# Squares summed ahead of the statistics matmul, the last weight tile loaded in pieces, and a reordered ending

## The reference

```python
for layer in range(2):                       # first block, 256 tokens
    mod = silu(c) @ ada_w[layer] + ada_b[layer]
    sh1, sc1, g1, sh2, sc2, g2 = split(mod, 6)
    h = modulate(rms_norm(x, mix_norm[layer]), sh1, sc1)
    y = ab_mixer(h) if layer == 0 else cd_mixer(h)     # each ends in: mix @ w_out
    x = x + g1 * y
    h = modulate(rms_norm(x, ffn_norm[layer]), sh2, sc2)
    x = x + g2 * swiglu(h, ffn_w1[layer], ffn_w2[layer])

h = concatenate([meta_tokens, x])            # second block, 16 + 256 = 272 tokens
proj = rms_norm(h, mix_norm_g) @ w_in
attn, conv = diff_attention(...), gated_conv(...)
h = h + concatenate([attn, conv]) @ w_out
h = h + expert_choice_ffn(rms_norm(h, ffn_norm_g), w_router, w_gate, w_up, w_down)
return rms_norm(h, final_norm_g)[:, 16:, :]

def rms_norm(t, w):
    return t * rsqrt(mean(t * t, axis=-1) + 1e-6) * w
```

## Time and profile before

| | |
|---|---|
| median of 3 runs | 1895.21 us (1893.5, 1895.21, 1895.69) |
| the profiled execution | 1902.33 us, with a span of 1900.9 us |
| TensorE busy | 1677.1 us, 88% of the span |
| TensorE weight load busy | 1007.9 us, 53% |
| VectorE busy | 634.5 us, 33% |
| ScalarE busy | 373.4 us, 20% |
| GpSimd busy | 32.4 us, 2% |
| moved by DMA | 577.30 MB, mean 304 GB/s |

### The profile page before, as it was taken

The page is one execution under the profiler, slowest core; times in us unless marked ns, Lnnn a source line. Parts: engine busy times, 40 slices in busy tenths (PEclk is TensorE's granted clock), DMA queues, the critical chain, the costliest instruction groups (busy, mean ns, idle before and its releaser), DMA issues.

```text
span 1900.9 us, 20565 instructions
## 1 busy us (share of the span) xinstructions
PE 1677.1 (88%) x8771; PEld 1007.9 (53%) x8771; DVE 634.5 (33%) x1227; ACT 373.4 (20%) x648; POOL 32.4 (2%) x39
## 2 busy tenths in 40 slices
PE   3998899999889999999799988898888878888877
PEld 2775699997679999657533322233222222222222
DVE  6567277755747554253300100101001010010102
ACT  2213243432433433041101000000000000000001
POOL 0101000000000000100010000000000000000000
PEclk7989889999999999999889998999889899999999
DMA  9554248745647545222569999999999999999995
GB/s 397 232 213 181 106 175 331 256 169 207 241 155 263 184 175 222 89 89 89 221 259 415 427 430 431 422 404 424 431 431 421 431 430 424 431 422 428 431 429 231
DMA packets 43739, 577.30 MB, mean 304 GB/s; under 512 B 4721, under 2 KB 6786, under 8 KB 7298
## 3 DMA queue, kind: packets, MB, share of 16 engines
q1 hardware_dynamic: 43650, 576.00, 74.0%
HBM read 574.93 MB, written 1.05 MB: 303 GB/s over the span
## 4 chain that ended last, share of the span: by engine, by line
PE 67%; DMA 22%; DVE 8%; ACT 2%; issue 1%; SPq 0%; DVEq 0%; ACTq 0%
DMA RING_T<-in_w_up 20%; PE P L989 18%; PE P L416 13%; PE P L1010 5%; PE P L697 4%; PE P L698 4%; PE P L699 4%; PE P L718 2%; PE P L717 2%; PE P L716 2%; PE P L967 2%; PE P L425 2%; DVE RING_T L1555 2%; PE P L1026 2%; DMA RING_T<-in_ada_w 1%; PE P L443 1%
## 5 line engine op out<-in xcount | busy, mean ns | idle before, releaser
L989 PE MATMUL P<-RING_T,SCR 128*34 128x512 f32 x1008 | 483.9, 637 | 118.6 <-DMA RING_T<-in_w_up 118.6
L990 PE MATMUL P<-RING_T,SCR 128*34 128x512 f32 x992 | 477.8, 639 | 0.0
L989 PEld LDWEIGHTS P<-RING_T,SCR 128*34 128x34 f32 x1008 | 114.6, 119 | 435.4 <-issue 434.8
L2097 DVE TENSOR_TENSOR SCR<-P,SCR 34x512 f32<-34x512 f32 x64 | 44.4, 693 | 772.4 <-ACT SCR L1464 772.4
L1010 PE MATMUL P<-RING_T,SCR 128*34 128x512 f32 x512 | 227.9, 594 | 10.6 <-DMA RING_T<-in_w_down 10.6
L1011 PE MATMUL P<-RING_T,SCR 128*34 128x512 f32 x512 | 227.9, 594 | 0.0
L697 PE MATMUL P<-SCF 128*128 128x256 f32 x704 | 205.1, 291 | 15.7 <-DVE SCF L1828 11.1
L416 PE MATMUL P<-HWC,RING_T 128*128 128x256 f32 (+1 forms) x832 | 196.9, 395 | 7.9 <-ACT HWC L1108 4.1
L698 PE MATMUL P<-SCF 128*128 128x256 f32 x704 | 202.8, 288 | 0.0
L699 PE MATMUL P<-SCF 128*128 128x256 f32 x704 | 202.6, 288 | 0.0
L416 PEld LDWEIGHTS P<-HWC,RING_T 128*128 128x128 f32 x832 | 161.7, 196 | 40.6 <-issue 14.1
(11 more groups left out here) (245 smaller groups left out, 1732.8 us busy)
## 6 DMA issues: line engine op xcount, KB each, us to landing
RING_T<-in_w_down SPq DMA_DIRECT2D x64, 2048.0 KB, 13.7
RING_T<-in_w_gate SPq DMA_DIRECT2D x63, 2048.0 KB, 16.7
RING_T<-in_w_up SPq DMA_DIRECT2D x62, 2048.0 KB, 12.2
RING_T<-in_ada_w SPq DMA_DIRECT2D x24, 2048.0 KB, 10.2
RING_T<-in_ffn_w SPq DMA_DIRECT2D x22, 2048.0 KB, 8.5
RING_T<-in_ffn_w SPq DMA_DIRECT2D x22, 1024.0 KB, 4.9
RING_T<-in_ab_w_in SPq DMA_DIRECT2D x7, 2048.0 KB, 18.0
RING_T<-in_w_in SPq DMA_DIRECT2D x6, 2048.0 KB, 8.4
```

Of the source, the lines that this page charges most:

```text
L989: pe.matmul(u.t[0:CAP, :], xs, wg.v(KC, 512)[:, c, :], start=c == 0, stop=c == KC - 1)
L990: ins = pe.matmul(u.t[64:64 + CAP, :], xs, wu.v(KC, 512)[:, c, :], start=c == 0, stop=c == KC - 1)
```

## The change

Six things change.

1. In the three output projections, VectorE adds up the squares of chunks 0 to 6 in `H[:, 0]`, one addition behind each residual from the third on, and TensorE multiplies ones with that sum and with the square of chunk 7 after the last chunk (`pe_out_stat`). `PeStat` is no longer used there, and no bank is held.
2. The last down tile of the last expert is loaded by four DMAs of 512 KB, each with its own semaphore, and the last four pairs of matmuls wait for one piece each.
3. For all experts, VectorE copies the right half of the result to `Y` in ScalarE's place.
4. The last combination and its residuals work on 256 columns instead of 272.
5. ScalarE's last table load is issued before its copy of the last expert's result, in place of after the last square.
6. VectorE multiplies each chunk of the final `X` with the norm's weight into a new buffer `XF` as soon as the chunk is there, and after the reciprocal root three products (four, three and one chunk) and three output transfers follow.

```diff
+FINAL = ((0, 4), (4, 7), (7, 8))
+OUT_STATS = ["ffn0", "ffn1", "ffn2"]
...
+        self.XF = s.take(KC, T, at=s.at)
...
-def pe_out_proj(nc, k, name, keys, mix, n, stat):
+def pe_out_stat(nc, k, name, c0):
+
+    u = pe_bank(nc, k, ("rms", name))
+    nc.tensor.wait_ge(k.sem["squares"], 6 * OUT_STATS.index(name) + 6)
+    nc.tensor.matmul(u.t[:, 0:L - c0], k.cc("ones"), k.H[:, 0, c0:L], start=True, stop=False)
+    nc.tensor.wait_ge(k.sem["square"], SQ[name] + KC)
+    nc.tensor.matmul(u.t[:, 0:L - c0], k.cc("ones"), k.H[:, KC - 1, c0:L], start=False, stop=True).then_inc(u.full, 1)
+
+
+def pe_out_proj(nc, k, name, keys, mix, n):
     for i in range(2):
         w = k.ring[keys[i]]
         nc.tensor.wait_ge(w.sem, w.n)
         for j in range(4):
             u = pe_chunk(nc, k, (name, "out", 4 * i + j), w.v(KC, 512), j, mix, n)
-            stat.upto(min(max(4 * i + j - stat.lag, 0), KC) if 4 * i + j < 7 else 7)
         w.left = (u.full, u.n)
-    stat.upto(KC)
...
-    stat = PeStat(nc, k, "ffn0", M)
-    stat.lag = 2
...
-    pe_out_proj(nc, k, "ab", [("abo", 0), ("abo", 1)], v.MIX, T, stat)
+    pe_out_proj(nc, k, "ab", [("abo", 0), ("abo", 1)], v.MIX, T)
+    pe_out_stat(nc, k, "ffn0", M)
...
     def down(e, i, u):
         w = ring["d", e, i]
-        pe.wait_ge(w.sem, w.n)
+        pieces = (e, i) == (E_N - 1, 3)
+        if not pieces:
+            pe.wait_ge(w.sem, w.n)
         t = P["eturn", e, i]
         pe.wait_ge(t.taken, t.done)
         for c in range(4):
+            if pieces:
+                pe.wait_ge(s[f"last{c}"], 16)
...
-            pe.matmul(u.t[:, 0:L], v.Y[0:NP, g % 2, c * 128:(c + 1) * 128], v.OGT[0:NP, g, :], start=True, stop=True).then_inc(u.full, 1)
+            c0 = M if stat else 0
+            pe.matmul(u.t[:, 0:L - c0], v.Y[0:NP, g % 2, c * 128:(c + 1) * 128], v.OGT[0:NP, g, c0:L], start=True, stop=True).then_inc(u.full, 1)
...
+        if e == E_N - 1:
+            act_table(nc, SET_EXP)
+
         u, g, r = P["eo", e], e // 2, 64 * (e % 2)
...
         act.activation(v.Y[r:r + CAP, g % 2, 0:512], u.t[0:CAP, :], ACT.Copy).then_inc(u.taken, 1)
-        act.activation(v.Y[r:r + CAP, g % 2, 512:1024], u.t[64:64 + CAP, :], ACT.Copy).then_inc(u.taken, 1)
     for c in range(KC):
         act_square(nc, k, M, c, P["comb", 7, c])
-    act_table(nc, SET_EXP)
     act_stat(nc, k, "fin", M)
...
-def dve_out_proj(nc, k, name, n, c0, gate):
+def dve_out_proj(nc, k, name, n, c0, gate, stat):
+
+    s, done = k.sem, 6 * OUT_STATS.index(stat)
     for c in range(KC):
         u = k.banks[name, "out", c]
         nc.vector.wait_ge(u.full, u.n)
         dve_residual(nc, k, u, u.t[:, 0:n], c, c0, gate)
+        if c >= 2:
+            nc.vector.wait_ge(s["square"], SQ[stat] + c)
+            if c > 2:
+                nc.vector.wait_ge(s["squares"], done + c - 2)
+            nc.vector.tensor_tensor(k.H[:, 0, c0:L], k.H[:, 0, c0:L], k.H[:, c - 1, c0:L], ALU.add).then_inc(s["squares"], 1)
...
+    def weighed(c):
+
+        u = P["comb", 7, c]
+        dve.wait_ge(u.taken, u.done)
+        dve.tensor_scalar(v.XF[:, c, :], k.X[:, c, M:L], k.vv("fin", c, c + 1), None, ALU.mult).then_inc(s["weighed"], 1)
+
...
-    combine(7)
+        u, g, r = P["eo", e], e // 2, 64 * (e % 2)
+        dve.wait_ge(u.full, u.n)
...
+        dve.tensor_copy(v.Y[r:r + CAP, g % 2, 512:1024], u.t[64:64 + CAP, :]).then_inc(u.taken, 1)
+    for c in range(KC):
+        u = P["comb", 7, c]
+        dve.wait_ge(u.full, u.n)
...
+        dve_residual(nc, k, u, u.t[:, 0:T], c, M, None)
+        if c:
+            weighed(c - 1)
+    weighed(KC - 1)
     dve_stat(nc, k, "fin", M)
-    dve_normed(nc, k, "fin", M, k.vv("fin"))
+    dve.wait_ge(s["weighed"], KC)
+    dve.wait_ge(s["rs"], rms_done("fin"))
+    for a, b in FINAL:
+        dve.tensor_tensor(v.XF[:, a:b, :], v.XF[:, a:b, :], bc(k.RS[:, 0:1, 0:T], b - a, T), ALU.mult).then_inc(s["final"], 1)
...
+    w = k.ring["d", E_N - 1, 3]
+    sp.wait_ge(*w.prev.left)
+    for c in range(4):
+        sp.dma_start(w.t[:, c * D:(c + 1) * D], A["w_down_2"][E_N - 1, 3][:, c * D:(c + 1) * D]).then_inc(s[f"last{c}"], 16)
     od = k.out.rearrange("p (k t) -> p k t", k=KC)
-    for c in range(0, KC, 4):
-        sp.wait_ge(s["hn"], HN["fin"] + c + 4)
-        sp.dma_start(od[:, c:c + 4, :], k.H[:, c:c + 4, M:L]).then_inc(s["out"], 16)
-    sp.wait_ge(s["out"], 32)
+    for n, (a, b) in enumerate(FINAL):
+        sp.wait_ge(s["final"], n + 1)
+        sp.dma_start(od[:, a:b, :], k.ex.XF[:, a:b, :]).then_inc(s["out"], 16)
+    sp.wait_ge(s["out"], 16 * len(FINAL))
```

More of the change, by code:

```diff
@@ L225 @@
 SEMS = [
-    "vecs", "cond_in", "ones_in", "consts", "x", "pos", "narrow", "small", "gup", "later", "poolw", "ex0", "ex1", "ex2", "out",
-    "cond", "ada", "mod", "xr", "xr_p", "sa", "square", "ln", "rs", "hs", "hn",
+    "vecs", "cond_in", "ones_in", "consts", "x", "pos", "narrow", "small", "gup", "later", "poolw", "ex0", "ex1", "ex2", "last0", "last1", "last2", "last3", "out",
+    "cond", "ada", "mod", "xr", "xr_p", "sa", "square", "squares", "ln", "rs", "hs", "hn",
     "angle", "trig", "g1one", "iwt", "gate_a", "gate_d", "decay_a", "decay_d", "cosm", "rope", "qeke", "kdqd", "atzero", "at", "relu", "score",
@@ L238 @@
     "lam_d", "lam_a", "dcos", "drope", "amax", "aexp", "asoft", "osq", "osub", "onorm", "czero", "conv",
-    "wkzero", "rmax", "rexp", "raff", "rtop", "rmask", "rank", "onehot", "ogzero", "og", "yzero", "esilu", "edown",
+    "wkzero", "rmax", "rexp", "raff", "rtop", "rmask", "rank", "onehot", "ogzero", "og", "yzero", "esilu", "edown", "weighed", "final",
 ]
@@ L790, in pe_cd @@
         pe.matmul(u.t[:, 0:T], v.PW[:, g, :], v.W4[g][:, g, M:L], start=True, stop=True).then_inc(u.full, 1)
-    stat = PeStat(nc, k, "ffn1", M)
-    stat.lag = 2
     for i in range(4):
@@ L796, in pe_cd @@
         pe.wait_ge(P["pooled", i].taken, P["pooled", i].done)
-    pe_out_proj(nc, k, "cd", [("cdo", 0), ("cdo", 1)], v.MIX, T, stat)
+    pe_out_proj(nc, k, "cd", [("cdo", 0), ("cdo", 1)], v.MIX, T)
+    pe_out_stat(nc, k, "ffn1", M)
 def pe_diff(nc, k):
@@ L899, in pe_diff @@
         chunk("cb", j)
-    stat = PeStat(nc, k, "ffn2", 0)
-    stat.lag = 0
     pe.wait_ge(s["onorm"], 4)
@@ L905, in pe_diff @@
         pe.wait_ge(t.taken, t.done)
-    pe_out_proj(nc, k, "diff", [("o2", 0), ("o2", 1)], v.MIX, L, stat)
+    pe_out_proj(nc, k, "diff", [("o2", 0), ("o2", 1)], v.MIX, L)
+    pe_out_stat(nc, k, "ffn2", 0)
 def pe_experts(nc, k):
@@ L1786, in dve_ab @@
     dve.wait_ge(s["mod"], ADA_AT[0, 5] + 1)
-    dve_out_proj(nc, k, "ab", T, M, k.gate(0, 0))
+    dve_out_proj(nc, k, "ab", T, M, k.gate(0, 0), "ffn0")
 class DveLow:
@@ L1919, in dve_cd @@
     dve.wait_ge(s["mod"], ADA_AT[1, 5] + 1)
-    dve_out_proj(nc, k, "cd", T, M, k.gate(1, 0))
+    dve_out_proj(nc, k, "cd", T, M, k.gate(1, 0), "ffn1")
 def dve_diff(nc, k):
@@ L2030, in dve_diff @@
         convolved(j)
-    dve_out_proj(nc, k, "diff", L, 0, None)
+    dve_out_proj(nc, k, "diff", L, 0, None, "ffn2")
 def dve_experts(nc, k):
@@ L2125, in dve_experts @@
         turned(e, 3)
-    combine(7)
+        u, g, r = P["eo", e], e // 2, 64 * (e % 2)
+        dve.wait_ge(u.full, u.n)
+        if e == 0:
+            dve.wait_ge(s["yzero"], 1)
+        if g >= 2:
+            t = P["comb", g - 2, KC - 1]
+            dve.wait_ge(t.full, t.n)
+        dve.tensor_copy(v.Y[r:r + CAP, g % 2, 512:1024], u.t[64:64 + CAP, :]).then_inc(u.taken, 1)
+    for c in range(KC):
+        u = P["comb", 7, c]
+        dve.wait_ge(u.full, u.n)
+        if c == 0:
+            t = P["comb", 6, KC - 1]
+            dve.wait_ge(t.taken, t.done)
+        dve_residual(nc, k, u, u.t[:, 0:T], c, M, None)
+        if c:
+            weighed(c - 1)
+    weighed(KC - 1)
     dve_stat(nc, k, "fin", M)
-    dve_normed(nc, k, "fin", M, k.vv("fin"))
+    dve.wait_ge(s["weighed"], KC)
+    dve.wait_ge(s["rs"], rms_done("fin"))
+    for a, b in FINAL:
+        dve.tensor_tensor(v.XF[:, a:b, :], v.XF[:, a:b, :], bc(k.RS[:, 0:1, 0:T], b - a, T), ALU.mult).then_inc(s["final"], 1)
 def vector_program(nc, k):
```

3 lines of the change are left out of this document (2 added, 1 removed).

## The result

| | before | after |
|---|---|---|
| median of the runs on one chip, 15 each | 1897.18 us (1893.5 to 1905.92) | 1890.46 us (1885.91 to 1894.94) |
| ratio to the kernel before | 1 | 0.9963 (0.9950 to 0.9976) |
| profiled execution, span | 1902.33, 1900.9 us | 1893.83, 1892.5 us |
| TensorE, VectorE, ScalarE busy | 1677.1, 634.5, 373.4 us | 1671.0, 652.6, 363.9 us |

The ratio is 7.0 us faster (9.5 to 4.6), where 8.0 were forecast. The first three runs of before, on which the forecast stood, happened to be short ones: with 15 the median is 2 us higher.

A forecast was written before the change was run, and what follows sets the result against it. TensorE and serial chains bound the kernel until about 960 us, then the experts' weight stream. Eight terms sum to 8.0 us, taken off the median 1895.21: 1887.2 us, own range 1885.3 to 1890.0, wide range 1884.3 to 1891.6.

The forecast's parts named there:

- ab: First output projection: four statistics fewer between chunks, 1.73 us, less 0.26 for a longer tail; net gain 1.47 us.
- cd: Second output projection: same pattern and distances as the first, gain 1.47 us again.
- diff: Third output projection: six statistics fewer, 2.73 us, less 0.36 for a longer tail; net gain 2.37 us.
- pieces: Last expert's last down tile in four DMAs: TensorE's idle time before it goes, gain 1.09 us.
- half the copy on VectorE: Last expert's result: VectorE's copy runs beside ScalarE's, so the combination starts earlier; gain 0.52 us.
- 256 columns, weighing: Last combination on 256 columns, weights multiplied in alongside: eight times 0.03, gain 0.24 us, bounds -0.7 to +0.24.
- table load: ScalarE's last table load moved ahead of its last copy: worth 0.0 us, as VectorE's read sets the logarithm's start.
- end: From reciprocal root to span's end: three final products and a smaller last output transfer, gain 0.83 us, bounds 0.6 to 1.5.
- What is saved on any engine between 980 and 1874 us is worth nothing: Experts' weight stream: DMA alone sets the time there, so engine savings inside it gain 0 us.
- The restart: Issue that restarts the experts' weight stream: to move from 966.43 to near 961.1; prediction wrong if not by about 5.
- two clock rivals: TensorE's low clock near the first expert: lasts longer, slower than before (3%); or 8 us shorter, 1883.2 us (5%).

The follow-up runs named there:

- squares only: Kernel before with only VectorE's additions of squares in the three output projections, ending as before; ratio 0.9972, 5.3 us faster.
- dose in diff: Kernel before with six extra matmuls ahead of each of the eight chunks of the third output projection; ratio 1.0110, 20.9 us slower.

## Why the prediction was right

The time, 1890.46, lies inside the range, and the gain of 7.0 us is near the 8.0. Step by step, by local rows:

| step | forecast | measured at its place |
|---|---|---|
| ab | 1.47 | 1.35 (1.73 less 0.38) |
| cd | 1.47 | 1.36 |
| diff | 2.37 | 2.32 |
| pieces | 1.09 | 0 to 0.9, by execution |
| half the copy on VectorE | 0.52 | 0.50 (1.89 to 1.39 from the last matmul's start to the combination's) |
| 256 columns, weighing | 0.24 | 0.22 (7.45 to 7.23) |
| table load | 0.0 | 0.01 |
| end | 0.83 | 0.85, with the final products in 2.43 us, not 2.60 |

The small miss in the projections is TensorE's restart after its pause: the second closing matmul follows the first by 0.51 and 0.54 us, not 0.43 and 0.46, and the first starts 0.07 to 0.08 late. The sum of the places is 6.6 to 7.5, and 7.0 was measured. That the total agrees so well is in part luck. Its interval is 2.4 us to either side, and two shifts of about 1 us, for which the sum has no term, work against each other: feed-forward 1 is longer, and the cd column is shorter by 2.2 us (111.25 against 113.4) in four of the seven profiles with the changed kernel's code there, where 1.36 is the projection's. What makes the rest of cd shorter was not tested.

Two steps of the text were wrong. "What is saved on any engine between 980 and 1874 us is worth nothing" took a DMA share of 1.00 for a hard bound with TensorE slack behind it all the way. Added work there costs 0.73 us per us (0.54 to 0.90); for saved work, which the sentence is about, the gain was 3.4 of 20 us and can't be told from nothing. This did no harm, because the change moves none of TensorE's work in the stream. And the piece term read one execution's wait of 0.93 us as a property of the kernel. The whole tile in the changed kernel costs nothing that the totals can tell.

The restart moved by 2.3 instead of 5, which the prediction had named as a sign of being wrong. The test was badly chosen. The first 232 us, nearly all of them ahead of the change, varied from 226.9 to 233.7 us between profiles, and the difference of neighbouring marks (cd, diff) shows what the absolute mark hides. The two clock rivals had the right kind of effect and too large a size: low stretches do shift in stages whose own code is unchanged, but by 1.2 us in feed-forward 1, not by 8 to 30 us.

## What to carry to other kernels

A statistic over a finished tensor costs a matrix engine that is the bound one matmul a chunk. Adding the squares on an idle engine takes that to two, here a sum and the last chunk. Leaving the last two chunks to the matrix engine saved 0.4 us more at each place, since it no longer waits for the last addition. Before pricing "the last tile in pieces" by its matmuls, look how long the engine idles before that tile, in more than one execution. And where a serial chain leaves the matrix engine idle just before work that it bounds, look at the granted clock behind the pause: filling the pauses gave about 4 us in the feed-forward parts and 3.6 in the router stage, by the rows of these places, which is more than any single step of the change.

## What was not expected

- Keeping TensorE busy with useless matmuls in pauses of 5.5 and 2.5 us kept the clock at 2.4 GHz, and shortened the feed-forward parts of some 208 us by 1.5 and 2.5 against their usual values. In the router stage 13 us at 1.2 GHz stayed, with TensorE busy all the time.
- 20.6 us of TensorE work added to a stream whose DMA share reads 1.00 cost 15.0 us; the moved bytes fell from 424 to 413 GB/s in one window of 60 us, and by 1% over the stream.
- The stream from restart to last read took 920.0 to 927.6 us in three profiles with the same code in that part (before, squares only, dose in diff).
